# State-space products in pairs of row groups and column groups, around half projection tiles

## The reference, cut to what matters

```
z = x @ w_in;   u, q, k, v, gate_s, gate_a = split(z)      # u: 1024 channels, q, k, v: 1536 each
ug = u.reshape(.., 64 groups, 16)
bu = einsum('blgh,gph->lbgp', ug, bb)                      # complex: 64 states for each group of 16 channels
h  = associative_scan(h[t] = abar * h[t-1] + bu[t])        # complex, 4096 states
y  = einsum('lbgp,ghp->blgh', h_re, c_re) - einsum('lbgp,ghp->blgh', h_im, c_im) + d_skip * u
g  = gelu(y);  out = g * sigmoid(g @ w_glu)
```

## Time and profile before

| | us |
|---|---|
| median of 3 runs (lowest, highest) | 3008.89 (3007.49, 3010.33) |
| profiled execution, device time | 3005.91 |
| its span, first to last instruction | 3003.6 |
| PE, DVE, POOL, ACT busy in the span | 2506.8, 1363.4, 867.0, 173.4 |
| mean granted TensorE clock | 0.952 |

### The profile page before, as it was taken

How to read it: one execution, slowest core, us unless ns; L and a number is a source line. 1 busy time by engine, 2 the same in 40 slices (tenths; PEclk the granted TensorE clock), 3 DMA queues, 4 the chain that set the end, 5 groups by cost and what they waited for, 6 DMA issues and landing times.

```text
span 3003.6 us, 26684 instructions
## 1 busy us (share of the span) xinstructions
PE 2506.8 (83%) x8982; PEld 1366.6 (45%) x8982; DVE 1363.4 (45%) x2340; ACT 173.4 (6%) x336; POOL 867.0 (29%) x844
## 2 busy tenths in 40 slices
PE   9998999969999999797677777776777777777798
PEld 6555567656777767564233333332223332322222
DVE  7666751100000000289566666666655555555421
ACT  0111111110000000300000000000000000000000
POOL 0111100000000000033555555554555554444431
PEclk9999899989999999898899999998999999999999
DMA  5221255774333333286999999999999999999995
GB/s 200 91 75 64 91 195 222 309 284 179 127 138 127 140 119 119 86 324 260 408 420 422 422 420 422 422 421 389 420 419 422 421 422 422 422 422 417 422 401 172
DMA packets 122269, 876.85 MB, mean 292 GB/s; under 512 B 14624, under 2 KB 17696, under 8 KB 19168
## 3 DMA queue, kind: packets, MB, share of 16 engines
q0 software_dynamic: 92160, 671.13, 54.3%
q1 hardware_dynamic: 30048, 204.93, 18.4%
HBM read 868.37 MB, written 6.85 MB: 291 GB/s over the span
## 4 chain that ended last, share of the span: by engine, by line
PE 42%; DMA 30%; DVE 15%; issue 10%; POOL 2%; DVEq 1%; ACT 1%; SPq 0%; POOLq 0%; ACTq 0%
PE ps L501 27%; DMA arena<-in_peer_u,arena 26%; PE ps L864 10%; DVE arena L1485 4%; DMA arena<-in_cache_b 3%; POOL arena L1182 2%; PE ps L660 1%; PE ps L548 1%; PE ps L539 1%; DVE arena L1436 1%; DVE arena L1446 1%; DVE arena L1432 1%; DVE arena L1448 1%; DVE arena L1290 0%; DVE arena L1460 0%
## 5 line engine op out<-in xcount | busy, mean ns | idle before, releaser
L864 PE MATMUL ps<-arena 128*128 128x512 f32 (+1 forms) x2560 | 1179.8, 612 | 395.9 <-DVE arena L1498 394.0
L501 PE MATMUL ps<-arena 128*128 128x320 f32 x3712 | 1032.2, 439 | 4.3 <-DVE arena L1396 1.8
L1485 DVE CUSTOM_DVE_ANT_0 arena<-arena 128x2048 f32<-128x2048 f32 x320 | 731.8, 2292 | 574.3 <-DMA arena<-in_peer_u,arena 571.6
L864 PEld LDWEIGHTS ps<-arena 128*128 128x128 f32 (+1 forms) x2560 | 456.1, 184 | 1119.6 <-issue 1119.4
L501 PEld LDWEIGHTS ps<-arena 128*128 128x128 f32 x3712 | 711.3, 193 | 314.4 <-issue 34.3
L1182 POOL DMA_INDIRECT arena<-in_peer_u,arena x320 | 394.7, 1233 | 683.5 <-DVE arena L1485 612.2
L1182 POOL DMA_INDIRECT arena<-in_peer_v,arena x320 | 372.7, 1165 | 164.2 <-issue 90.0
L1173 POOL COPY arena<-arena 128x8 int32 (+1 forms) x80 | 58.6, 732 | 657.2 <-DVE arena L1463 647.7
L1395 DVE TENSOR_TENSOR arena<-arena,ps 128x640 f32<-128x640 f32 x16 | 13.1, 821 | 357.6 <-PE ps L501 357.6
L1498 DVE TENSOR_SCALAR arena<-arena 128x128 f32<-128x128 f32 (+1 forms) x320 | 87.9, 275 | 91.2 <-PE ps L864 91.1
L1127 POOL COPY arena<-arena 128x18 f32 x32 | 8.7, 273 | 299.7 <-DVE arena L1297 299.7
(11 more groups left out here) (196 smaller groups left out, 951.7 us busy)
## 6 DMA issues: line engine op xcount, KB each, us to landing
arena<-in_w SPq DMA_DIRECT2D x128, 1024.0 KB, 4.8
arena<-in_cache_b SPq DMA_DIRECT2D x16, 2048.0 KB, 9.5
arena<-in_cache_a SPq DMA_DIRECT2D x16, 1280.0 KB, 8.0
arena<-in_peer_u,arena POOLq DMA_INDIRECT x320, 16.2
arena<-in_peer_v,arena POOLq DMA_INDIRECT x320, 17.7
out_kv<-arena SPq DMA_DIRECT2D x4, 960.0 KB, 11.6
arena<-in_xT SPq DMA_DIRECT2D x4, 640.0 KB, 7.7
arena<-in_ln SPq DMA_DIRECT2D x2, 1024.0 KB, 5.9
```

What stands on the lines that cost most here:

```text
L501: ins = pe.matmul(out, lhs(k), rhs(k), start=(k == 0), stop=(k == n - 1))
L864: ins = pe.matmul(ps[0:rows, b0 + q, :], diag[:, e % DIAGS, 0:rows], vb[v][:, q * 512:(q + 1) * 512], start=False, stop=True, skip_group_c ...
L1485: dve.tensor_tensor_reduce(ub[k], ub[k], htok[:, a, :], 1.0, 0.0, ALU.mult, ALU.add, act_[:, place, e:e + 1]).then_inc(u_used, 1)
```

## The change

The loops of the stage are written out in full on SyncE, TensorE, ScalarE and VectorE (GpSimd keeps its loop), so waits compare with constants. The tiles of the stage get a new order, `SSM_ORDER`: the u tile of the next quad comes between the two other tiles of a quad. TensorE's order in a quad is now: a tile; input products 2 and 3 as a pair; the first half (8 matmuls) of the next quad's u tile; output products 0 and 1 as a pair; the second half; the transposes of the next B; the first half of the second tile; input products 0 and 1 of the next quad; its second half; output products 2 and 3. In a pair the matmuls alternate: real part of both state tiles, then imaginary part of both. VectorE computes the skip term of a quad after the first state tile of the next one, and scales the next B after the second state tile instead of the third. ScalarE's order follows: u and B are staged between the two evacuations of other tiles, the evacuation of the second tile stands ahead of the next quad's first magnitude row, and Gelu of a quad comes in the middle of the next. SyncE waits for the B and C of a quad after the first of its tiles in place of the last. The packing of the weights follows the new order, and the ninth, unused scaling, transposing and staging of B are gone.

```diff
+SSM_ORDER = [("u", 0)]
+for _q in range(QUADS):
+    SSM_ORDER += [("head", 2 * _q)] + ([("u", _q + 1)] if _q + 1 < QUADS else []) + [("head", 2 * _q + 1)]
+SSM_AT = {t: n for n, t in enumerate(SSM_ORDER)}
...
# SyncE
+            for m, (kind, x) in enumerate(SSM_ORDER):
+                sp.wait_ge(used, N_PRE + m - RING + 1)
+                w(N_PRE + m)
+                if kind == "head" and x % 2 == 0 and x // 2 + 1 < QUADS:
+                    q = x // 2
+                    sp.wait_ge(bb_ready, q + 1)
+                    sp.dma_start(braw, A["ssm_b"][q + 1]).then_inc(b_in, 16)
+                    sp.wait_ge(cc_ready, q + 1)
+                    sp.dma_start(craw, A["ssm_c"][q + 1]).then_inc(c_in, 16)
...
# TensorE
-            def tile(i, k):
-                pe.wait_ge(wsem[k % RING], i * (3 * BODY // RING * 16) + 16 * ((N_PRE + k) // RING + 1))
-                pe.wait_ge(evac, i * (3 * BODY) + (N_PRE + k - 1))
-                project(k % RING, k % 2).then_inc(used, 1)
+            def tile(kind, x, parts=(0, 1)):
+                m = SSM_AT[kind, x]
+                n = N_PRE + m
+                if 0 in parts:
+                    pe.wait_ge(wsem[n % RING], 16 * (n // RING + 1))
+                    pe.wait_ge(evac, n - 1)
+                s = slot(n % RING)
+                for t in range(min(parts) * KT // 2, (max(parts) + 1) * KT // 2):
+                    ins = pe.matmul(ps[:, n % 2, 0:T], s[:, t, :], xT[:, t, :], start=(t == 0), stop=(t == KT - 1))
+                if 1 in parts:
+                    ins.then_inc(used, 1)
...
+            def b_u(q, j):
+                pe.wait_ge(bt_ready, q + 2)
+                pe.wait_ge(evac, N_PRE + SSM_AT["u", q] + 1)
+                pe.wait_ge(bu_free, q * PER_QUAD + (j + 2))
                 for part in range(2):
+                    for i in (j, j + 1):
+                        lo = 32 * i
+                        ins = pe.matmul(ps[:, 2 + 2 * (i % 2) + part, 0:T], btq[lo:lo + 32, part, :],
+                                        uq[lo:lo + 32, q % 2, :], start=True, stop=True)
+                        if part:
+                            ins.then_inc(bu_ready, 1)
             def c_h(q, j):
+                pe.wait_ge(cc_ready, q + 1)
+                pe.wait_ge(ypre_ready, q + 1)
+                pe.wait_ge(h_ready, q * PER_QUAD + (j + 4))
                 for part in range(2):
+                    for i in (j, j + 1):
+                        lo = 32 * i
+                        ins = pe.matmul(ps[lo:lo + 32, 6, 0:T], ccq[:, part, lo:lo + 32], hs[:, i % 2, part, :],
+                                        start=(part == 0), stop=(part == 1))
+                        if part:
+                            ins.then_inc(y_done, 1)
             b_transposed(0)
+            tile("u", 0)
+            b_u(0, 0)
+            for q in range(QUADS):
+                last = q + 1 == QUADS
+                tile("head", 2 * q)
+                b_u(q, 2)
+                mid = ("head", 2 * q + 1) if last else ("u", q + 1)
+                tile(*mid, (0,))
+                c_h(q, 0)
+                tile(*mid, (1,))
+                if not last:
+                    b_transposed(q + 1)
+                    tile("head", 2 * q + 1, (0,))
+                    b_u(q + 1, 0)
+                    tile("head", 2 * q + 1, (1,))
+                c_h(q, 2)
...
# ScalarE
+            stage_u(0)
+            for q in range(QUADS):
+                mag_row(q, 0)
+                mag_row(q, 1)
...                               # C staged as before
+                stage_head(2 * q)
+                if q:
+                    stage_g(q - 1)
+                mag_row(q, 2)
+                mag_row(q, 3)
+                if q + 1 < QUADS:
+                    stage_u(q + 1)
+                    stage_b(q + 1)
+                stage_head(2 * q + 1)
+            stage_g(QUADS - 1)
...
# VectorE
+            def skip_term(q):
+                dve.wait_ge(y_done, q * PER_QUAD + (PER_QUAD + 2))
+                dve.wait_ge(g_ready, q + 1)
+                STT(ypre, uq[:, q % 2], dskip[:, q:q + 1], ps[:, 6, 0:T], ALU.mult, ALU.add).then_inc(ypre_ready, 1)
+            for q in range(QUADS):
+                states(q, 0)
+                if q:
+                    skip_term(q - 1)
+                states(q, 1)
+                if q + 1 < QUADS:
+                    dve.wait_ge(h_ready, q * PER_QUAD + 4)
+                    scale_b(q + 1)
+                states(q, 2)
+                states(q, 3)
+            skip_term(QUADS - 1)
```

More of the change, by code:

```diff
@@ L87 @@
 N_SSM = N_PRE + 3 * QUADS
-BODY = 4
+SSM_ORDER = [("u", 0)]
+for _q in range(QUADS):
+    SSM_ORDER += [("head", 2 * _q)] + ([("u", _q + 1)] if _q + 1 < QUADS else []) + [("head", 2 * _q + 1)]
+SSM_AT = {t: n for n, t in enumerate(SSM_ORDER)}
+assert N_PRE + len(SSM_ORDER) == N_SSM
 FILL = 4
@@ L543, in c_h @@
             def c_h(q, j):
-                lo = 32 * j
-                pe.wait_ge(h_ready, q * PER_QUAD + (j + 3))
+                pe.wait_ge(cc_ready, q + 1)
+                pe.wait_ge(ypre_ready, q + 1)
+                pe.wait_ge(h_ready, q * PER_QUAD + (j + 4))
                 for part in range(2):
-                    ins = pe.matmul(ps[lo:lo + 32, 6, 0:T], ccq[:, part, lo:lo + 32], hs[:, j % 2, part, :],
-                                    start=(part == 0), stop=(part == 1))
-                ins.then_inc(y_done, 1)
@@ L552, in _ @@
-            b_transposed(0)
[L553 to L570, removed]
+                    for i in (j, j + 1):
[4 more added lines that the diff above has]
+                            ins.then_inc(y_done, 1)
@@ L572, in _ @@
+            b_transposed(0)
+            tile("u", 0)
[9 more added lines that the diff above has]
+                if not last:
                     b_transposed(q + 1)
-                    if k < BODY - 1:
-                        tile(i, 3 * k + 3)
@@ L575, in _ @@
-                    c_h(q, 3)
+                    tile("head", 2 * q + 1, (0,))
+                    b_u(q + 1, 0)
+                    tile("head", 2 * q + 1, (1,))
+                c_h(q, 2)
             def heads_tile(f):
@@ L904, in stage_b, with stage_u @@
                                ACT.Copy).then_inc(bt_ready, 1)
[L906 to L916, removed]
+            def stage_u(q):
+                act.wait_ge(used, N_PRE + SSM_AT["u", q] + 1)
+                act.wait_ge(ypre_ready, q)
+                evacuate(uq[:, q % 2], SSM_AT["u", q] % 2)
@@ L918, in _, with stage_head, stage_g @@
+            def stage_head(x):
+                m = SSM_AT["head", x]
+                act.wait_ge(used, N_PRE + m + 1)
+                evacuate(qkv[:, N_PRE + x, :], m % 2)
+            def stage_g(q):
+                act.wait_ge(ypre_ready, q + 2)
+                act.activation(gT[:, q, :], ypre, ACT.Gelu_apprx_tanh).then_inc(g_ready, 1)
             act.wait_ge(su_act, 1)
             stage_b(0)
[L920 to L933, removed]
-                    stage_b(q + 1)
[L935 to L939, removed]
@@ new lines, in _ @@
+            stage_u(0)
+            for q in range(QUADS):
+                mag_row(q, 0)
+                mag_row(q, 1)
+                act.wait_ge(c_in, q * 16 + 16)
+                act.wait_ge(y_done, q * PER_QUAD + 2)
+                act.activation(ccq[:, 0, :], craw[:, 0, :], ACT.Copy)
+                act.activation(ccq[:, 1, :], craw[:, 1, :], ACT.Copy, scale=-1.0).then_inc(cc_ready, 1)
+                stage_head(2 * q)
[5 more added lines that the diff above has]
+                    stage_u(q + 1)
+                    stage_b(q + 1)
+                stage_head(2 * q + 1)
@@ L1312, in _ @@
             scale_b(0)
[L1313 to L1319, removed]
-                    scale_b(q + 1)
[L1321 to L1326, removed]
+            def skip_term(q):
[9 more added lines that the diff above has]
+                    dve.wait_ge(h_ready, q * PER_QUAD + 4)
+                    scale_b(q + 1)
+                states(q, 2)
+                states(q, 3)
+            skip_term(QUADS - 1)
             dve.wait_ge(fin_done, STILES + 2)
@@ L1617, in lay_out @@
     order = list(heads[:N_PRE])
-    for q in range(QUADS):
-        order += [u[q], heads[N_PRE + 2 * q], heads[N_PRE + 2 * q + 1]]
+    order += [u[x] if kind == "u" else heads[N_PRE + x] for kind, x in SSM_ORDER]
     order += list(heads[O_FILL:])
```

6 lines of the change are left out of this document (removed).

## The result

The changed kernel takes 2935.2 us (median of 4, 2926.2 to 2936.4) against 3009.6 before (median of 4). The ratio is 0.9747, 95% interval 0.9726 to 0.9767: 2.5% faster, 74 us. The prediction said 2940 in a range of 2929 to 2975. The profiled execution takes 2935.8 (span 2933.5).

The account below looks back on a forecast made before the run. TensorE bound the kernel's stage; afterwards VectorE's cycle would, at 32.2 us a quad. Stage end 346.3 instead of 418.4: 72.1 saved less 3 for clock, 69; profiled 2937, median 3.0 above: 2940, range 2929 to 2975.

Parts of the forecast that it names:

- pairs: TensorE: input pairs at 1.28 save 10.2 us, output pairs at 1.20 save 19.2; rival, column pairs queue: 2953, chance 0.17.
- waits and clock: TensorE in the stage: 53 us of waits and slow clock go; rival, a wait and slow clock stay: 2977, chance 0.17.
- the end: Last quad: TensorE idle about 8.5 us before state 3 is written, then slow clock taken as 3, bounds 0 to 5.
- VectorE's chain: VectorE per quad: states of 7.05, scaling 1.57, skip term 0.6, a late table; cycle 32.0, just over TensorE's 31.7.
- wait for GpSimd's table: VectorE at a quad's first state: rotation table copied by GpSimd comes 1.6 us later than VectorE would start.
- the constants: Constants in place of loop registers: nothing on TensorE or VectorE; bounds -0.3 to +0.3 us a quad.
- the two engines catching on each other: TensorE and VectorE in each quad: 0.2 us added to the cycle of 32.0, giving 32.2.
- table load before the first u: ScalarE at the stage's start: the load of 1.28 us goes, 1.3 saved.
- The magnitude row: ScalarE, state 0: the row stands behind the head tile's evacuation but stays hidden by 3 us.
- The weights: SyncE's queue: tiles hidden by 4 us, at worst 0.8 late, taken as 0; rival, late landing: 3016, chance 0.03.
- It moves up whole: Rest of the kernel: it starts from this stage's end, so all of it moves up with the stage.
- signs of being wrong: Quads over 34 apart, the lower clock back inside the stage, or the stage after it giving back more than 5 us.

Follow-up runs that it names:

- Run 4: Changed kernel with both output products of a pair in one column group and both input products from one row group: 2969.0 us.
- 11: Changed kernel with half the first attention-stage tile in the idle before the last output pair and first cached keys loaded early: 2930.6 us against 2937.2.
- run 7: Changed kernel with whole tiles in place of the halves around output pair 0 and the next quad's input pair 0: 2933.0 us.
- run 6: Kernel before, written out, with products in pairs at the places of before: 3008.0 us against 3010.5, ratio 0.9985.
- run 1: Kernel before with its stage loops written out, order of work unchanged: 3003.9 us against 3009.9, ratio 0.9981.
- run 9: Changed kernel with two more VectorE instructions in each quad but the last, ahead of the scaling of B: 2943.5 us.
- run 8: Changed kernel with output pair 0 moved straight behind input pair 2, the second tile whole behind it: 2948.5 us.

## Why the prediction was right

**The account.** On the chip of runs 4 and 11 the changed kernel gains 73.2. Run 4 divides this into 41.4 without any sharing and 31.8 for the sharing; that the two add up is no check, since one is the rest of the other. Written out is 6.1, measured on another chip, which leaves 35.3. But the kernel before had 8 of the 32 pairs already. At 1.07 each they are 8.6 of the 31.8, so for the change I estimate some 23 for its 24 new pairs and 44 for the order. The prediction had 29.4 for pairs and 53 for waits and clock, less 15 for the end and small waits, and 1.6 for the start and the skip term.

**Pairs.** Right in mechanism and price. 1.20 for columns (argued from the earlier trace rows) and 1.28 for rows (from the earlier trace rows) were measured as just that. Halves were put at nothing and cost 0.25 a quad (run 7). The Trainium skill's sentence on weight loads (TensorE: Matmul & The Clock Gate, The mechanism) does not hold for column groups here: eight loads in groups that share all rows pass within the pair's 1.20 (from 137.62 to 138.31, beside the pair's row at 137.62). What the prediction didn't say is that pairing is worth its price only where TensorE does not wait behind it (run 6).

**Waits and clock.** Right: no idle on TensorE above 0.6 in the stage but the last, clock 0.99.

**VectorE's chain.** The step that was mis-sized. I took 32.0 a quad for its cycle; it is 31.2. The new wait for GpSimd's table came as costed (1.6 plus 0.14, measured 1.75), but two terms were too large. A state takes 6.93, not 7.05: the 0.15 of idle before the short addition is gone, in run 1 too. It stands in this row of the kernel before:

```profile
263.37 0.19 DVE L1287 TENSOR_TENSOR arena<-arena 128x16 f32<-128x16 f32 x1 [0.15 <-DVE arena L1284]
```

"Nothing on TensorE or VectorE", said the prediction of the constants; it was 0.12 a state, 0.5 a quad. And the skip term adds 0.25 between two states (7.18 against 6.93) where I took 0.6. So TensorE, with 31.8, is the longer of the two in a quad, where I had VectorE. The stage gained 77.1 where I had 72.1, and VectorE's chain shows where: first state 0.2 sooner, first quad 0.4 shorter, the next six 188.1 instead of 193.2, the last 0.3 shorter, and 1.0 more for the output pair at the lower clock. My 0.2 a quad for the two engines catching on each other, 1.2 in sum, is in the 193.2; measured are 0.8 there and 0.6 in the last quad, all as waits for the magnitude row.

**ScalarE and SyncE.** The table load before the first u went as said (first pair at 89.95, forecast 90.2). The magnitude row was not hidden by 3 us: in the last three quads TensorE's tile comes late against VectorE, and the scan waited 1.4 for it in sum. VectorE has no other slack up to the last output pair, which waits for it, so these 1.4 are in the stage's length. That they would go with the row ahead of the evacuation I didn't test. The weights never came late.

**The end.** 4.8 of idle instead of 8.5, again since VectorE was sooner. The slow clock behind it cost 1.1 in the pair, and 1.6 of lead were gone by the merge; 3 were allowed for both.

**Downstream.** "It moves up whole" was wrong by 5.3 us: 3.4 between layer norm and expert stage, 1.9 in the expert stage. The same step exists in two lengths, 87.5 and 90.8 from the last residual to the first dot product: 87.5 or 87.6 before and in runs 1 and 7, 90.7 to 91.0 in the changed kernel and in all other runs. So the new order has been seen with the short one (run 7) and the old order with the long one (run 6). There is one profiled execution of each kernel and two of the changed one, which is too few to say that the change has no part in it. It hangs on the variance matmuls behind 2.88 of idle, in run 7 and in the changed kernel:

```profile
1134.50 8.88 PE L815 MATMUL ps<-arena 128*128 128x320 f32 x32 [2.88 <-ACT arena L1051]
```

```profile
1136.91 11.94 PE L817 MATMUL ps<-arena 128*128 128x320 f32 x32 [2.88 <-ACT arena L1053]
```

The same idle, once with the clock up behind it and once with it down. What the 1.9 us in the expert stage are I didn't test. From the first dot product to the last matmul group the profiles of all kernels here, which are the same in that stage, take 1700.9 to 1707.2.

The stage gave 5.0 more than forecast, and the rest of the kernel took back 6.9 where 3 were allowed. The two misses nearly cancelled: 70.1 of the profiled execution against a forecast of 69 is in part luck. Of my signs of being wrong, none came inside the stage. The stage behind it gave back 1.6, the rest of the kernel in all more than the 5 that I had named for that stage.

## What to carry to other kernels

Ask of each term in a sum whether its engine sets the pace at that point: 24 pairs that would save 26 us at their measured price saved nothing where TensorE waited behind them for VectorE's result (run 6). Place the product that feeds the other engine ahead of the one that waits for it (whole tiles between them will do); then pair products of different row or column groups side by side, in any order. Before filling an idle gap at a stage's end, look at what the next stage waits for.

## What the runs showed of the hardware

- Two row groups or two column groups run a pair of 8 records in the time of 4 (1.28 and 1.20 us); in one group it is 2.34 and 2.27.
- The clock behind an idle stretch is not decided by its length alone. It stayed up behind 2.04 (fifth quad before). Behind 2.88 it stayed up in three of the profiled executions and fell in the eleven others. It fell once behind 1.14 (run 9), where four of 1.10 in the same run and seven of 1.12 in run 8 passed.
- The written-out code took 0.12 us out of each of VectorE's state tiles (7.05 to 6.93), with ten instructions in each; that it is the waits on constants in place of loop registers I argue and didn't test apart.
- Eight weight loads of two column groups pass inside the 1.20 us of their pair (the first 0.7 of it).
